# Streaming a matmul's 512 tokens as two interleaved halves, in runs of 16, 64 and 4 columns

## The reference

```python
def conv_ffn(u, w_up, conv_w, conv_b, w_down):
    h = u @ w_up.astype(u.dtype)                    # (512, 1024) @ (1024, 5632)
    h = causal_depthwise_conv(h, conv_w, conv_b)    # width 3, along the tokens
    gate, val = jnp.split(h, 2, axis=-1)
    return (jax.nn.silu(gate) * val) @ w_down.astype(u.dtype)

for i in range(DEPTH):                              # DEPTH = 2
    h = rms_norm(x, norm_mix_pre[i])
    mix = ssd_mixer(h, ...) if i % 2 == 0 else pool_mixer(h, ...)
    x = x + rms_norm(mix, norm_mix_post[i])
    f = conv_ffn(rms_norm(x, norm_ffn_pre[i]), ffn_w_up[i], ...)
    x = x + rms_norm(f, norm_ffn_post[i])
```

## Time and profile before

| | |
|---|---|
| median of 3 runs | 1206.85 us (1205.99 to 1207.28) |
| profiled execution: its time | 1206.16 us |
| profiled execution: its span | 1204.4 us |
| TensorE busy | 1157.6 us, 96% of the span |
| VectorE, ScalarE busy | 671.7 us (56%), 523.0 us (43%) |
| mean granted TensorE clock | 0.991 of full |
| the two loops of up products (iterations 1 to 10) | 449.6 to 667.5 us and 856.1 to 1074.0 us |

### The profile page before, as it was taken

How to read it: one execution, slowest core, us unless ns; L and a number is a source line. 1 busy time by engine, 2 the same in 40 slices (tenths; PEclk the granted TensorE clock), 3 DMA queues, 4 the chain that set the end, 5 groups by cost and what they waited for, 6 DMA issues and landing times.

```text
span 1204.4 us, 14740 instructions
## 1 busy us (share of the span) xinstructions
PE 1157.6 (96%) x5780; PEld 965.7 (80%) x5780; DVE 671.7 (56%) x766; ACT 523.0 (43%) x613; POOL 32.6 (3%) x87
## 2 busy tenths in 40 slices
PE   5999999999999899999999999997999999999997
PEld 5877888888788688888888888887888888888885
DVE  4568777878642746556565422476556655562114
ACT  4466666667532544434444211354534444341112
POOL 5000000000100000000000000000000000000000
PEclk9999999999999899999999999999999999999999
DMA  8242343433223303333223332502232233323221
GB/s 276 62 133 86 121 137 113 137 111 135 90 70 105 105 8 134 103 104 104 90 84 104 105 105 81 174 9 70 88 105 85 91 103 104 104 72 109 99 70 70
DMA packets 85227, 122.26 MB, mean 102 GB/s; under 512 B 4150, under 2 KB 71198, under 8 KB 85182
## 3 DMA queue, kind: packets, MB, share of 16 engines
q1 hardware_dynamic: 84592, 121.37, 30.7%
q10 hardware_dynamic: 590, 0.25, 0.1%
HBM read 119.44 MB, written 2.16 MB: 101 GB/s over the span
## 4 chain that ended last, share of the span: by engine, by line
PE 90%; DVE 5%; ACT 3%; DMA 1%; issue 1%; SPq 0%; DVEq 0%; ACTq 0%
PE bank L874 25%; PE bank L269 19%; PE bank L271 19%; PE bank L270 19%; PE bank L646 2%; DVE w_lo L266 2%; PE bank L655 1%; ACT w_hi L261 1%; DMA raw<-in_ssd_w_in 1%; DVE stage L301 1%; DVE xres L304 1%; PE bank L1035 1%; PE bank L600 1%; PE bank L333 1%; PE bank L573 1%
## 5 line engine op out<-in xcount | busy, mean ns | idle before, releaser
L269 PE MATMUL bank<-h_hi,w_hi 128*128 128x512 f32 (+1 forms) x1056 | 403.4, 382 | 12.7 <-DVE h_lo L345 9.2
L271 PE MATMUL bank<-h_hi,w_lo 128*128 128x512 f32 (+1 forms) x1056 | 399.4, 378 | 0.0
L270 PE MATMUL bank<-h_lo,w_hi 128*128 128x512 f32 (+1 forms) x1056 | 399.0, 378 | 0.0
L266 DVE TENSOR_TENSOR w_lo<-raw,w_hi 128x2048 fp32r<-128x2048 f32 x92 | 210.8, 2291 | 244.1 <-ACT w_hi L261 243.8
L380 DVE SCALAR_TENSOR_TENSOR tmp<-bank,par,tmp 128x511 f32<-128x511 f32 (+2 forms) x248 | 185.2, 748 | 129.4 <-ACT tmp L371 116.5
L261 ACT ACTIVATE w_hi<-raw 128x2048 fp32r<-128x2048 f32 x92 | 175.3, 1905 | 175.0 <-PE bank L874 158.1
L269 PEld LDWEIGHTS bank<-h_hi,w_hi 128*128 128x128 f32 x1056 | 200.6, 190 | 51.0 <-DVE w_lo L266 7.2
L271 PEld LDWEIGHTS bank<-h_hi,w_lo 128*128 128x128 f32 x1056 | 200.4, 190 | 36.8
L270 PEld LDWEIGHTS bank<-h_lo,w_hi 128*128 128x128 f32 x1056 | 200.6, 190 | 35.1
L371 ACT ACTIVATE tmp<-bank,par 128x512 f32<-128x512 f32 x112 | 86.6, 774 | 259.4 <-PE bank L271 259.3
L874 PE MATMUL bank<-w_hi,act_hi 128*128 128x512 f32 x352 | 110.7, 395 | 0.0
(11 more groups left out here) (161 smaller groups left out, 964.4 us busy)
## 6 DMA issues: line engine op xcount, KB each, us to landing
raw<-in_ffn_w_up SPq DMA_DIRECT2D x44, 1024.0 KB, 5.1
raw<-in_ffn_w_down SPq DMA_DIRECT2D x22, 1024.0 KB, 5.0
raw<-in_ssd_w_in SPq DMA_DIRECT2D x20, 1024.0 KB, 5.6
decay<-ac_dram SPq DMA_DIRECT2D x16, 512.0 KB, 3.9
raw<-in_ssd_w_out SPq DMA_DIRECT2D x8, 1024.0 KB, 5.0
from_start<-ac_dram SPq DMA_DIRECT2D x32, 128.0 KB, 3.8
xres<-in_x SPq DMA_DIRECT2D x4, 512.0 KB, 8.1
result<-xres SPq DMA_DIRECT2D x4, 512.0 KB, 2.6
```

Of the source, the lines that this page charges most:

```text
L266: dve.tensor_tensor(lo[:], raw[n % 2][:], hi[:].bitcast(F32), ALU.subtract).then_inc(lo_ready, 1)
L269: pe.matmul(dst, wh, xh, start=first, stop=False, **kw)
L270: pe.matmul(dst, wh, xl, start=False, stop=False, **kw)
L271: return pe.matmul(dst, wl, xh, start=False, stop=last, **kw)
```

## The change

`block_product` takes a run length. With a run of `n` columns the moving operands and the bank are seen through `in_runs`: the 512 columns as two halves of 256, from which runs of n columns are taken in turn, first half, second half, first half and so on. The matmul still streams 512 columns, each column still lands in its own place of the bank, and the result is the same. In `up_pe` the four blocks of an iteration get runs of 16, 64, 4, and no runs. Nothing else calls `block_product` with a run.

```diff
+        def in_runs(ap, run):
+            return ap if run == T else ap.rearrange("p (a r n) -> p r a n", a=2, n=run)
+
-        def block_product(pe, dst, slot, j):
+        def block_product(pe, dst, slot, j, run=T):
             wh, wl, c = by_cols(w_hi[slot]), by_cols(w_lo[slot]), slice(j * P, (j + 1) * P)
             for k in range(DB):
-                mm = three_passes(pe, dst, wh[:, k, c], wl[:, k, c], h_hi[:, k, :], h_lo[:, k, :],
-                                  k == 0, k == DB - 1)
+                mm = three_passes(pe, in_runs(dst, run), wh[:, k, c], wl[:, k, c], in_runs(h_hi[:, k, :], run),
+                                  in_runs(h_lo[:, k, :], run), k == 0, k == DB - 1)
             return mm
...
+        UP_RUN = [16, 64, 4, T]
...
-                    block_product(pe, bank[:, 4 + q, :], (S_UP[l] + s) % 2, j).then_inc(blk_done, 1)
+                    block_product(pe, bank[:, 4 + q, :], (S_UP[l] + s) % 2, j, UP_RUN[q]).then_inc(blk_done, 1)
```

## The result

The changed kernel takes 1228.7 us in the median of four runs (1224.8 to 1232.9), the kernel before 1206.6 us in those beside it: a ratio of 1.018, 95% interval 1.015 to 1.022. It is slower by 22 us. The time lies inside the range that I gave (1197 to 1243), but the case that I called likeliest, no change, is not what happened.

The account below looks back on a forecast made before the run. TensorE was taken to bound the kernel, busy throughout both loops. Profiled execution 1206.16 us plus 1440 x 0 ns, named as the runs' median, 1206.9 us; range 1197 to 1243 us.

Parts of the forecast that it names:

- no change: Whole kernel: the patterned matmuls cost nothing more, 1206.9 us, own range 1204.5 to 1209.3, chance 0.56.
- TensorE alone bounds the loop, and a nanosecond per matmul moves the end by a nanosecond.: Both up-product loops: PE busy all 217.90 us, no slack; 1 ns longer per matmul moves the end by 1 ns.
- I count as nothing: TensorE's clock in the loops: a lower one would be another cause, given no size since the engine stays as busy.
- I take the value 0: Jumps in the 1440 patterned up-product matmuls: 0 ns each, as all rows with gaps lie there.
- rival 1: Patterned up products: each jump costs one array clock, 0.417 ns, 33.6 us in all, 1240.5 us; chance 0.12.
- Rival 2: Patterned up products: data's place matters, not the jump; up to 6.2 ns each, 8.9 us, up to 1215.8 us; chance 0.10.
- Rivals 3 and 4: Up products at half rate: shortest run alone, 1304 us, chance 0.06; or every gap in the bank, 1498 us, 0.09.
- rival 4: Patterned up products: every gap in the bank halves the rate, whatever the run; 291 us, 1498 us; chance 0.09.
- Rival 5: Up-product loop: another address order may miss a clash behind the 13.6 ns; down to 1187 us; chance 0.07.
- The two sentences of the Trainium skill: Patterned up products: by one, all 1440 would be slower; by the other, all three run lengths are free, sum 0.

Follow-up runs that it names:

- e9: The kernel before, with 32 unused bytes per partition ahead of the tiles of xbc, y and act; median 1199.5 us, ratio to before 0.9952.
- e10: The changed kernel with 32 unused bytes between h_lo and raw, so that all weight tiles move against h; 1241.4 us.

## Why the prediction came out as it did

- *TensorE alone bounds the loop, and a nanosecond per matmul moves the end by a nanosecond.* Right: 19.5 us in the loops, PE busy all the time, 18.6 us in the span (the first loop began 0.9 us earlier).
- *A lower clock "I count as nothing".* In the profiled run it was nothing: 1.00 in both loops. Two of the four runs had a lower mean clock and took some 7 us more, which puts 4 us into the median; the sum had no term for it.
- *"I take the value 0."* This is the step that failed. The patterned matmuls cost 13.3 (16), 1.6 (64) and 23.7 ns (4) more, and the straight 480 beside them 2.1. The rows that I leaned on were of the wrong operand and the wrong rate: L666 was the load port, L339 and L345 were engines that take over 1 ns a column. At half the rate the runs of 16 and 4 are free on TensorE too. The row that spoke against 0 was in the prediction too, as "for it" of rival 1: 256 more columns cost 111 ns where one clock a column makes 107, a stream with next to no slack.
- *Rival 1, one clock per jump, 1240.5 us.* It has the right sign and the right engine, and comes nearest of the slower cases, but its law is wrong: it put 76% of the loss on the 4s and 5% on the 64s; measured were 58% and, but for the neighbour's effect, none, and the price of a length changes with the distance of the jump. (n runs have n - 1 jumps inside a matmul, so its counts are each one too high, which changes little.)
- *Rival 2, the place matters, up to 6.2 ns.* Not what the change did (its tiles stay where they are), but a real and separate mechanism of 6.6 ns, shown by e9 and e10. I left the difference of the down products unexplained, and it was the one gain found here.
- *Rivals 3 and 4, half rate.* No length fell to it (429.2 ns); the 2s, which the change doesn't use, came to 339.2 ns. The bank side of rival 4 is refuted by the run with only the bank in runs.
- *Rival 5, faster through another order.* No order of the stream fell below 226.7 ns.
- *The two sentences of the Trainium skill.* "PSUM — Partial Sum Buffer", section Specifications (TRN2), says that any non-contiguous access in PSUM slows matmuls significantly; the run with only the bank in runs shows 226.7 ns with runs of 4 to 64, so the trace doesn't agree. "Advanced Engine Details and Errata", section Memory Cachelines, speaks of SBUF's lines of 16 bytes and the two hits that each needs. The step from runs of 4 (24 ns) to runs of 2 (113 ns) would fit such a line, though at two hits the 2s should have passed too; and filled lines weren't enough, since 4, 8, 16 and 32 fill them and pay 10 to 24 ns.

What stays open: why a jump costs what it does (10, 13, 17, 24 ns for 32, 16, 8, 4 with halves; 7, 7, 41 for 32, 16, 4 with quarters). The runs show that it is the reading of the stream at full rate, that the distance between the runs matters, and that 64 columns in a row are enough here. Whether a jump wastes fetches or costs a small delay of its own, and which address bits matter, was not found.

## What to carry to other kernels

The float32r stream of this kernel passes a column every 0.44 ns, close to one per clock, and its order isn't free even where every address is visited once. Keep 64 columns or more in a row in what is streamed, as was free here, and try a permutation on the bank's side, where interleaving in runs of 4 to 64 cost nothing. Where two stages with equal matmuls differ in their distance from start to start, compare where their streamed tile and their stationary tile begin: an idle 32 bytes gave 0.5% here. And a row of another engine, or of the other operand, didn't bound the price of a stream at full rate.

## What I had not expected of the hardware

- The price of a stream depends on the relative place of the weight load beside it: 226.7 ns at a multiple of 512 bytes from each other, 233 with 32 bytes off, shown by moving either tile.
- A load of 32 columns, or of one column again and again, went with a slower straight stream (231.7 ns), not a faster one.
- After a change of order some ten matmuls pass before the distance settles at 226.7 ns; a block of 24 loses some 46 ns by it (1.9 ns each).
- Gaps in the bank cost nothing, down to runs of 4 columns (226.7 ns).
- Runs of 2 columns cost 339.2 ns at the full rate and still 24 ns above straight at half the rate, where 429.2 ns would have been time enough for the same order.
